# One addition of every feed-forward unit moved ahead on VectorE, a first weight slot loaded in halves, and two norm borders reordered

## The reference, cut to what matters

```python
# first block, layer 0 (even), then layer 1 (odd)
y = even_mixer(h)        # h @ e_w_in, chunked mLSTM + compressed/selected/windowed attention, @ w_out
h = layer_norm(DN_ALPHA * h + y)
u = square(relu(h @ mlp_w1)) @ mlp_w2              # 1024 -> 4096 -> 1024
h = layer_norm(DN_ALPHA * h + u)
h = h + sigmoid(h @ ple_gate_w) * (p @ ple_w)
...                      # odd: odd_mixer (latent attention) in place of even_mixer
# second block, twice
x = x + 0.5 * (silu(n @ w_gate) * (n @ w_up)) @ w_down   # n = rmsnorm(x), 1024 -> 2816 -> 1024
x = x + mixer(rmsnorm(x)) @ w_out
x = x + 0.5 * swiglu(rmsnorm(x))                         # second feed-forward
...
return rmsnorm(x)
```

## Time and profile before

| | us |
|---|---|
| median of 3 runs | 3303.37 |
| lowest, highest | 3303.18, 3304.42 |
| the profiled execution's own time | 3302.54 |
| its span, first to last instruction | 3300.9 |
| PE busy in it | 3221.0 |
| DVE, ACT, POOL busy | 2011.2, 1440.8, 860.8 |

### The profile page before, as it was taken

The page is one execution under the profiler, slowest core; times in us unless marked ns, Lnnn a source line. Parts: engine busy times, 40 slices in busy tenths (PEclk is TensorE's granted clock), DMA queues, the critical chain, the costliest instruction groups (busy, mean ns, idle before and its releaser), DMA issues.

```text
span 3300.9 us, 47396 instructions
## 1 busy us (share of the span) xinstructions
PE 3221.0 (98%) x20089; PEld 2864.7 (87%) x20092; DVE 2011.2 (61%) x2885; ACT 1440.8 (44%) x2132; POOL 860.8 (26%) x381
## 2 busy tenths in 40 slices
PE   8999999999999999999999999999999999999998
PEld 6887899988668899889998878999989988888997
DVE  6568655454866544666666546666667466366755
ACT  4465454443443444444443334444445343234543
POOL 3210034321410233202322430242223233312322
PEclk9999999999999999999999999999999999999999
DMA  4310233331112333323322322332323323222322
GB/s 133 106 52 26 90 103 115 102 122 58 52 39 90 103 115 103 104 75 109 122 91 82 115 65 90 115 115 96 103 90 116 96 81 124 77 90 91 125 85 77
DMA packets 222915, 308.95 MB, mean 94 GB/s; under 512 B 7824, under 2 KB 151200, under 8 KB 222192
## 3 DMA queue, kind: packets, MB, share of 16 engines
q1 hardware_dynamic: 219120, 291.41, 26.6%
q0 software_dynamic: 3584, 14.52, 1.2%
HBM read 303.80 MB, written 2.10 MB: 93 GB/s over the span
## 4 chain that ended last, share of the span: by engine, by line
PE 74%; DVE 19%; ACT 4%; issue 2%; DMA 0%; POOL 0%; DVEq 0%; ACTq 0%
PE bank L603 23%; PE bank L605 22%; PE bank L604 22%; DVE wlo L2091 5%; ACT whi L1329 2%; DVE wraw L2113 1%; DVE raw_w L2113 1%; DVE ul_w L2297 1%; PE bank L986 1%; PE bank L623 1%; DVE zt L2292 1%; PE bank L1268 1%; PE bank L1259 1%; PE bank L1193 0%; DVE st L2122 0%
## 5 line engine op out<-in xcount | busy, mean ns | idle before, releaser
L3157 POOL TENSOR_TENSOR wlo<-wraw,whi 128x1024 fp32r<-128x1024 f32 (+1 forms) x199 | 525.6, 2644 | 1367.5 <-ACT whi L1329 1367.3
L603 PE MATMUL bank<-xh,whi 128*128 128x256 f32 (+1 forms) x2456 | 720.1, 293 | 30.9 <-DVE xl L2388 12.1
L1329 ACT ACTIVATE whi<-wraw 128x1024 fp32r<-128x1024 f32 (+2 forms) x398 | 435.6, 1098 | 644.1 <-PE bank L605 504.7
L605 PE MATMUL bank<-xh,wlo 128*128 128x256 f32 (+1 forms) x2456 | 715.8, 291 | 0.0
L604 PE MATMUL bank<-xl,whi 128*128 128x256 f32 (+1 forms) x2456 | 711.5, 290 | 0.0
L3157 POOL TENSOR_TENSOR wlo<-raw_w,whi 128x1024 fp32r<-128x1024 f32 x116 | 294.3, 2539 | 850.8 <-ACT whi L1329 850.8
L603 PEld LDWEIGHTS bank<-xh,whi 128*128 128x128 f32 x2456 | 463.5, 189 | 49.8 <-POOL wlo L3157 14.4
L603 PE MATMUL bank<-whi,uh_w 128*128 128x512 f32 x1216 | 474.4, 390 | 0.6 <-DVE ul_w L2706 0.6
L605 PE MATMUL bank<-whi,ul_w 128*128 128x512 f32 x1216 | 473.4, 389 | 0.0
L604 PE MATMUL bank<-wlo,uh_w 128*128 128x512 f32 x1216 | 473.2, 389 | 0.0
L604 PEld LDWEIGHTS bank<-xl,whi 128*128 128x128 f32 x2456 | 463.8, 189 | 10.4
(11 more groups left out here) (395 smaller groups left out, 4991.2 us busy)
## 6 DMA issues: line engine op xcount, KB each, us to landing
wraw<-in_w_in SPq DMA_DIRECT2D x26, 1024.0 KB, 5.0
wraw<-in_ffn_w_gate SPq DMA_DIRECT2D x40, 512.0 KB, 4.7
raw_w<-in_ffn_w_gate SPq DMA_DIRECT2D x40, 512.0 KB, 4.6
raw_w<-in_ffn_w_up SPq DMA_DIRECT2D x40, 512.0 KB, 4.3
wraw<-in_ffn_w_up SPq DMA_DIRECT2D x40, 512.0 KB, 4.3
wraw<-in_ffn_w_down SPq DMA_DIRECT2D x20, 1024.0 KB, 5.0
raw_w<-in_ffn_w_down SPq DMA_DIRECT2D x20, 1024.0 KB, 5.0
raw_w<-in_mlp_w SPq DMA_DIRECT2D x19, 1024.0 KB, 5.0
```

What stands on the lines that cost most here:

```text
L603: M.matmul(o, lh, rh, start=start, stop=False, skip_group_check=more)
L605: return M.matmul(o, ll, rh, start=False, stop=stop, skip_group_check=more)
L1329: A.activation(hi, raw, ACT.Copy).then_inc(*k.w_hi.inc(("hi", j)))
L3157: G.tensor_tensor(lo[:, 0:n], raw[:, 0:n], hi[:, 0:n].bitcast(F), ALU.subtract).then_inc(*k.w_lo.inc(("lo", j)))
```

## The change

The order of PE's instructions stays as it is apart from the first slot. The change does five things.

- DVE's `units` calls product 7 before `slots.get` in every unit (`ahead = p == 7`). In 34 units this moves the addition in front of one or two other instructions; in the rest nothing stands between.
- ACT's `units` calls product 1 of the second unit before `slots.get` in the first part of a stage; only the gated feed-forwards have a second unit there.
- In the last columns of `e_out` and `o_out`, ACT finishes the fourth part's slot and splits the next item before the norm of tile 2; DVE splits it between tiles 2 and 3.
- The first slot comes as two halves of 512 KB, with x's pieces between; their low parts, and those of four other slots of the even mixer, are made by DVE alone, others by POOL alone. PE does the first slot with k outside and both banks inside.
- The compression weights leave the slots: four loads of 512 KB directly behind the constants, into memory that is free then (`s.cmp`), and a memset of `vx` waits for PE's `hidden(0)`.

```diff
-        while self.ahead < len(self.plan) and max(self.plan[self.ahead].before + self.plan[self.ahead].behind, default=-1) < self.i:
+        while self.ahead < len(self.plan) and max(self.plan[self.ahead].before, default=-1) < self.i:
...
+    def halves(self, tag, view):
+
+        pair = self.pairs(1)[0]
+        for n in range(2):
+            load = self.load(view[:, 4 * n:4 * n + 4, :], [2 * pair + n])
+            self.loads[load].items = [self.item(tag, load, 1, 0, 4, "dve")]
...
-    add_fm("e_in", v, 0, 768)
+    plan.halves("e_in", v[:, :, 0:256])
+    plan.slot("e_in", v[:, :, 256:512], low="dve")
+    plan.slot("e_in", v[:, :, 512:768])
     plan.slot("e_g", v[:, :, 3328:3424])
-    add_fm("e_in", v, 768, 1024)
-    add_fm("e_vs", v, 1024, 1280)
+    plan.slot("e_in", v[:, :, 768:1024], low="dve")
+    plan.slot("e_vs", v[:, :, 1024:1280], low="dve")
     for j in range(2):
-        plan.slot("cmp", I["e_b_cmp_w1"][j].rearrange("p (k c) -> p k c", c=128))
-        add_fm("e_qk", v, 1280 + 256 * j, 1536 + 256 * j, share=True)
-    plan.items[-1].behind.append(len(plan.items) - 2)
+        plan.slot("e_qk", v[:, :, 1280 + 256 * j:1536 + 256 * j], low=("pool", "dve")[j])
...
# TensorE, the first slot
+        for kk in range(8):
+            if kk % 4 == 0:
+                wh, wl = weights(j + kk // 4)
+            pe.wait_ge(at("x", kk))
+            for m, key in enumerate(keys):
...
# ScalarE, last columns of a stage
+                if tag in ("e_out", "o_out"):
+                    slots.done()
+                    slots.prepare()
+                    then((*name, c, 2), c, 2)
+                else:
+                    then((*name, c, 2), c, 2)
+                    slots.done()
                 then((*name, c, 3), c, 3)
# ScalarE, units
+            ahead = first and (i, p) == (1, 1)
+            if ahead:
+                product(blocks[i], p)
             slots.get(tag)
             slots.done()
-            product(blocks[i], p)
+            if not ahead:
+                product(blocks[i], p)
# VectorE
                 then((*name, c, 2), c, 2)
                 slots.done()
+                if tag in ("e_out", "o_out"):
+                    slots.prepare()
                 then((*name, c, 3), c, 3)
...
-            ahead = first and (i, p) == (0, 7)
+            ahead = p == 7
...
         fm("e_in", [[("e_in", 4), ("e_in", 5)]], e_in)
-        windows(0)
         slots.skip("e_g", 1)
         slots.prepare()
+        windows(0)
...
# SyncE
-    load(0)
     for n in range(4):
+        if n % 2 == 0:
+            load(n // 2)
         S.dma_start(k.even.qk[:, 2 * n:2 * n + 2, :], ...
-    load(1)
+    load(2)
...
+    for n in range(2):
+        for half in range(2):
+            S.dma_start(k.even.cmp[n][half],
+                        I["e_b_cmp_w1"][n][:, half * 1024:half * 1024 + 1024]).then_inc(*k.landed["cmp"].inc(("cmp", n)))
```

More of the change, by code:

```diff
@@ L834, in hidden @@
             for kk in range(16):
-                i = M.matmul(bank[0:64, 0:128], blk[:, kk, :], w[:, kk, :], start=(kk == 0), stop=(kk == 15))
-            i.then_inc(*made.inc(("made", ("hidden", n)), ("used", j)))
-            slots.done()
+                i = M.matmul(bank[0:64, 0:128], blk[:, kk, :], w[kk // 8][:, kk % 8 * 128:kk % 8 * 128 + 128], start=(kk == 0), stop=(kk == 15))
+            i.then_inc(*made.inc(("made", ("hidden", n))))
         def hidden_features(n):
@@ L1321, in split @@
     def split(j):
-        if whole(k, j):
-            return
         item = k.plan.items[j]
@@ L1523, in even @@
         e = k.even
-        split(0)
-        slots.ahead = 1
-        for f in range(8):
-            act.wait_ge(at("xT", f // 2))
-            A.activation(xh[:, f, :], e.qk[:, f, :], ACT.Copy).then_inc(*done.inc(("x hi", f)))
+        for n in range(2):
+            split(n)
+            for f in range(4 * n, 4 * n + 4):
+                act.wait_ge(at("xT", f // 2))
+                A.activation(xh[:, f, :], e.qk[:, f, :], ACT.Copy).then_inc(*done.inc(("x hi", f)))
+        slots.ahead = 2
         def e_in(key):
@@ L1543, in e_in @@
                     A.activation(e.kh[other, i - 6, g, :], src, ACT.Copy).then_inc(*done.inc(("ks hi twice", i - 6, g)))
-        fm("e_in", [[("e_in", 2 * n), ("e_in", 2 * n + 1)] for n in range(3)], e_in)
+        slots.get("e_in")
+        e_in(("e_in", 0))
+        e_in(("e_in", 1))
+        slots.done(2)
+        fm("e_in", [[("e_in", 2 * n), ("e_in", 2 * n + 1)] for n in (1, 2)], e_in)
         slots.get("e_g")
@@ L1588, in hidden @@
         def hidden(n):
-            slots.get("cmp")
-            slots.done()
-            slots.prepare()
             key = ("hidden", n)
@@ L2264, in tm, with units @@
                 between()
-    def units(tag, blocks, product, finish, rest=iter(()), first=False):
+    def units(tag, blocks, product, finish, rest=iter(())):
         waiting = []
         for i, p in product_order(len(blocks)):
-            ahead = first and (i, p) == (0, 7)
+            ahead = p == 7
             if ahead:
@@ L2408, in e_in @@
                         ("ks split", i - 6), *([("free", key)] if g else [])))
-        fm("e_in", [[("e_in", 2 * n), ("e_in", 2 * n + 1)] for n in range(2)], e_in)
+        slots.get("e_in")
+        e_in(("e_in", 0))
+        e_in(("e_in", 1))
+        slots.done(2)
+        fm("e_in", [[("e_in", 2), ("e_in", 3)]], e_in)
         dve.wait_ge(at("con"))
@@ L3151, in split @@
         item = k.plan.items[j]
-        if whole(k, j) or item.low == "dve":
+        if item.low == "dve":
             return
@@ L3201, in even @@
         e = k.even
-        split(0)
-        slots.ahead = 1
-        G.memset(e.vx[:, :, :, 128:130], 1.0).then_inc(*done.inc(("vx ones",)))
+        slots.ahead = 2
         G.dma_start(e.w2, I["w2"]).then_inc(*k.landed["w2"].inc(("w2",)))
-        slots.skip("e_in", 3)
+        slots.skip("e_in", 4)
         slots.skip("e_g", 1)
@@ L3213, in even @@
         slots.done()
-        for n in range(2):
-            slots.skip("cmp", 1)
-            slots.skip("e_qk", 1)
+        slots.skip("e_qk", 2)
+        pool.wait_ge(at("made", ("hidden", 0)))
+        G.memset(e.vx[:, :, :, 128:130], 1.0).then_inc(*done.inc(("vx ones",)))
         pool.wait_ge(at("hc", 1))
```

67 lines of the change are left out of this document (32 added, 35 removed).

## The result

The changed kernel takes 3315.2 us (median of 6 runs, 3313.3 to 3316.0); beside it the kernel before takes 3303.8 (6 runs, 3303.2 to 3305.1). The ratio is 1.0033, with a 95% interval of 1.0021 to 1.0045. I had forecast 3288 and a range of 3280 to 3296: the change makes the kernel slower by 11 us instead of faster by 15. One execution of a later experiment (`e12_copy_back`) took 4511 us at a granted clock of 0.65 and is left out of its median.

A forecast was written before the change was run, and what follows sets the result against it. PE bounds the kernel, busy 3221.0 of 3300.9 us, so only its idling and clock can give time. 5.1 - 0.6 + 7.1 - 1.0 + 4.4 = 15.0 us gained, forecast 3288 us, range 3280 to 3296.

The forecast's parts named there:

- The start: First slot: the first matmul comes at 7.8 instead of 12.14, a gain of 4.3 us.
- The even mixer: Even mixer, from the first slot through the hidden features: a gain of 5.1 us, of which 4.3 is the start.
- The new wait at the third slot: Even mixer: PE waits 0.8 us for POOL's low part of the third slot, bounds 0 and 1.5.
- the operation that I had named: Even mixer: DVE's 4-row L2462, held by POOL until 76.3, so PE starts the first `e_qk` product at 79.1.
- The later waits: Even mixer: waits of 2.08 us for the second `e_qk` slot and 0.96 for the second gelu go.
- the slow stretch at 54.7: Even mixer: lower clock behind the wait before `e_in` 6, 24 matmuls in 7.02 us instead of 5.57; 1.4 us goes.
- my 0.6 for the clock: Even mixer: 0.6 us taken off the gain for what the waits do to the clock.
- The borders: Behind `e_out` and `o_out`: earlier low parts gain 1.4 us and 3.0 us, 4.4 in all.
- The units: Feed-forward units: a gain of 7.1 us from both edits less 1.0 for the later chain, 6.1 us.
- The 3.8 us for the 8-chunks' waits for `zt`: Gated feed-forwards' smaller waits for product 7's addition: 8 x 0.47 = 3.8 us, all gained.
- the allowance: Units: 1.0 us taken off, bounds 0 and 5, for DVE's later chain in the eight up-to-gate passages.
- The wait for product 7 costs more than it gives: slower: Rival, 34 units: later weight work makes PE wait before product 6 or 5, 0.5 us a unit, 3305 us; chance 0.04.

The follow-up runs named there:

- e12_copy_back: The faster version with GpSimd's wait (3282.1 us), without ACT's early copy of product 1 in a first part: 3284.2 us.
- e9_bank_first: VectorE's eight splits into `kl` moved ahead of the held 4-row operation, on the faster version with GpSimd's wait (3282.1 us): 3278.57 us, ratio 0.9923.
- e3_copy_alone: The kernel before with one edit, ACT's copy of product 1 of a first part's second unit ahead of the next high part: 3304.99 us, ratio 1.0001.

## Why the prediction was wrong

The rows of PE in the changed kernel on which the next three points rest, and the window behind `o_out`:

```profile
7.97 0.77 PE L603 MATMUL bank<-xh,whi 128*128 128x512 f32 x1 [7.97 <-DVE xl L2414]
...
87.12 0.27 PE L857 MATMUL bank<-con,an_e 64*128 64x64 f32 x1
...
1042.70:1052.70 10.00, 9.37 (x81) 9.17 (x80) 8.45 (x13) 4.53 (x10) 0.00 (x0) 1.00 0.32 107
```

**The start: right.** The first matmul is at 7.97 (forecast 7.8), so 4.2 us are gained (4.3).

**The even mixer: right.** The new wait at the third slot is 0.3 instead of 0.8. The first `e_qk` product begins at 79.73 (79.1) after a wait of 3.52 for `kl`, behind an operation held by POOL (L2492, the one before the operation that I had named), and the hidden features at 87.1 (86.7). The later waits and the slow stretch at 54.7 are gone. The forecast up to the units of mlp 0 was 5.1 - 0.6 + 1.4 (`e_out`) = 5.9, and the gain there is 6.7. The clock does fall behind the wait for `kl`: the 24 matmuls from 79.73 to 87.12 take 7.39 us at a granted clock of 0.77, where 24 take 5.57 at full clock. But that costs nothing, since ACT's gelu, for which PE would have waited, ends only at 87.07; the slow stretch stands where I had forecast a wait of 2 us, and my 0.6 for the clock was not needed. The rule of the Trainium skill ("SBUF — State Buffer", "Who interferes with whom"), that VectorE's operations with two inputs in SBUF are held and those with one are not, is borne out on both sides by the rows of `e9_bank_first` and the changed kernel: 4.98 us for a 4-row operation of the one kind, 0.68 for each split, which is of the other, beside the same POOL operation.

**The borders: right.** Forecast 4.4; taking them out costs 5.5, of which 4.5 are at the borders. PE waits 0.64 before tile 3's transposes behind `e_out` (forecast 0.9), and the low clock behind `o_out` is gone (1.00 in the window), and is back when the order is (0.84): 3.1 us gained in the odd part, forecast 3.0. That a wait of 2.05 us brings the low clock isn't certain, though: behind `e_out` the matmuls and transposes take 9.22 us at full clock before, and 10.81 at 0.84 in `e3_copy_alone`, where nothing was changed there.

**The units: wrong, and all of the miss.** Forecast +6.1; measured -20.6 (the windows above). The part of it that I gave the first parts was 0.84 each and is 1.13 (PE waits 0.56 us for POOL there before product 2, where I had 1.0 to 1.2); nearly all of that is product 7's, since a first part takes 90.9 us with its edit alone and 90.8 with the copy's too. The 3.8 us for the 8-chunks' waits for `zt`, "all gained", didn't come: the eight waits of 0.47 in the third units are gone, and eight of 0.76 stand in the fourth. The step that failed is the allowance behind "Following it through, product 6's low part is ready 2.1 us before PE after a gate unit, and 0.6 after an up unit", for which I took off 1.0 us with a bound of 5. It failed in three places.

- I followed the delayed chain to product 6's low part and to ACT's copy of product 1. The tightest link is one product further on: the copy of product 6, two high parts deep in ACT's queue, with 1.3 us to spare against a delay of 2.1. With the up units' additions, and nothing held, the loss is 15.5 us.
- I moved DVE's chain by 2.2 us and kept every duration. But POOL's operations did not all move with it, and where a sum came to stand behind one, it took 2.2 us more. I had used just this hold in the even mixer, priced it right there, and did not look for it in the units, where 16 sums that were free before are held now. POOL's wait shows the size of all that was held: 12.7 us, some 11.5 of it in the 8-chunks. Nor did I see that the kernel before had 9 held sums, four of them behind the first parts' waits for `zt`.
- I took the allowance for the eight up-to-gate passages only. The plain feed-forwards got nothing, with no reason given, and lose 5.5 us, by waits for ACT's copies.

The rival "The wait for product 7 costs more than it gives: slower" named the mechanism in part (3305, at 0.5 us a unit in 34 units, with PE before product 6 or 5) and had 0.04. It is 2.5 us in each of eight chunks and 2 to 3 in each plain feed-forward, and at products 6, 7 and 4. What I held against it, that PE waits there nowhere before, says nothing of how near it is to waiting. The bound of 5 us that I set for the passages had no row behind it.

## What to carry to other kernels

An in-order engine that is made to stand for an event before it does other work delays all that is queued behind it; the slack to check is that of every link on every engine for two or three steps ahead, not of the first one that PE asks for. When one chain is shifted against another, write down anew which operations of VectorE with both inputs in SBUF now start inside one of GpSimd's: the duration in the trace holds only for the order in the trace. A held operation costs only where its chain has nothing to spare: of the 9 in the kernel before, five cost nothing, and four cost a wait of 1.0 us each. And an edit like this is best made only where the trace shows its wait: in the first parts and in the third unit of each 8-chunk it gave 6.2 us, in all units it took 21.9; with GpSimd made to wait for that sum and the bank freed first, the kernel is at 3278.6 instead of 3303.5.

## What the runs showed of the hardware that was not expected

- A wait added to an engine that has time can make a kernel faster: GpSimd's low part begins behind VectorE's sum, and 12.7 us come back. In the kernel before, the same wait frees 9 sums and gives some 2 us by the stages, too little for the medians (3302.87 against 3303.53).
- A short wait costs more than the list says. In the first 8-chunk the list has four waits in the changed kernel, 0.49, 0.75, 0.26 and 0.76 us, and one of 0.47 before: 1.8 us more, of the 2.49 measured. The other 0.7 is in PE's busy time (80.66 against 79.96 for the same matmuls), some 0.2 for each wait more. Most of that is how a wait is counted: matmuls of 0.28 us follow each other every 0.12, so 0.16 of a stop lies under the record of the matmul before it; and the first one behind a wait takes 0.36, with 0.19 to the next start.
- The clock was not part of this: in the windows of the units it is 1.00 before and after.
